# Moving the split weight buffers by 128 bytes in a decoder-layer kernel

## The chip, the core and the metric

The kernel runs on one core of one Trainium2 chip. The metric is the device time of one execution in microseconds (us). TensorE does the matmuls, VectorE (DVE), ScalarE (ACT) and GpSimd (POOL) the elementwise work, SyncE (SP) issues most of the DMAs. All of them read their operands from SBUF, a memory of 128 partitions; where a buffer starts in the bytes of a partition is what is changed here.

## The reference

One hybrid decoder layer over 256 tokens of width 2048, in float32:

```python
proj = h @ w_in                                  # q, k, v, two latents, rope, two gates
y_a = dilated_window_attention(q, k, v) @ a_w_out
y_b = mla_attention(cq @ w_uq, ckv @ w_ukv) @ mla_w_out
mix = (g_a * y_a + g_b * y_b) @ w_out
h = layer_norm(ALPHA * h + mix)
# PEER: product keys choose 16 of 128*128 experts per head, 8 heads
u = expert_down[e];  v = expert_up[e]
y = sum over chosen e of  gate_e * gelu(u . h) * v
h = layer_norm(ALPHA * h + y)
```

The kernel doesn't gather experts. It computes `gelu(h @ down)` for all 16,384 experts, multiplies it by a gate matrix that is zero except at the chosen ones, and multiplies the product by `up`.

## The kernel before, in words

All weights come as one stream of 425 tiles of 128 x 2048 float32, in the order in which they are used: 64 tiles for q, k, v and one gate of each head, 9 for the latents, 16 for the other gate, 32 for the second attention and the first output projection, 16 each for the second output projection, the mixing projection and the query projection, 128 for the down table and 128 for the up table. Each tile is loaded in two halves of 128 x 1024. There are four slots for halves, in three buffers: `raw` is filled by SP's DMA, ScalarE rounds it into `w_hi` (type fp32r) and VectorE writes the rest, `raw - w_hi`, into `w_lo` (line 666). Each slot takes 4096 bytes of a partition.

A product in float32 is made of three fp32r products: hi x hi, lo x hi and hi x lo. In all stages but the last the weights are the stationary operand (128 x 128, loaded by LDWEIGHTS, "PEld" in the profile) and the activations move (256 columns, 258 in the query projection): `three`, line 1115, called 16 times per tile by `full` and 16 times by `up_proj`. That makes 297 tiles x 48 = 14,256 matmuls; these stages are called the dense ones below. In the up stage it is the other way round: the gated activations `m_hi` and `m_lo` are stationary, and 512 columns of `w_hi` or `w_lo` move (`up`, line 1320, and `up_bank` for the last two tiles); that makes 128 x 24 = 3,072 matmuls. Three neighbours in program order differ in which of the three products they are, not in their size. Between the tiles of the attention stages stand the small float32 matmuls and transposes of one head (lines 1149 to 1170).

The order of work is written out by hand for each engine, with semaphores between them. Buffers are laid out in the order of their declaration, each behind the one before. From the sizes follows where each starts. Modulo 512 bytes these places are, before: `raw`, `w_hi`, `w_lo` at 128; `a_hi`, `a_lo`, `res`, `cst` at 64; with the spacer `gap_b` behind `cst`, all buffers of the later stages that TensorE reads (`b_hi`, `b_lo`, `c_hi`, `c_lo`, `head`, `logit`, `p_t`, `v_t`, `qp`, `keys`, `r_hi`, `r_lo`, `m_hi`, `m_lo`) at 64 too. Every operand of a matmul starts a whole multiple of 512 bytes behind the start of its buffer, so these numbers hold for each of them.

Of the kernel before, what the change touches and what calls it, by code (L numbers as in the profile page):

```python
# [24 lines left out]
F32 = mybir.dt.float32  # L25
# [6 lines left out]
P = 128  # L32
# [11 lines left out]
TOPK = 16  # L44
# [32 lines left out]
C_ID = C_ROPE + T  # L77
C_ONE = C_ID + P
C_IOTA = C_ONE + P
C_SLOPE = C_IOTA + P  # L80
C_TOKEN = C_SLOPE + HEADS
N_CONST = C_TOKEN + 16

# [24 lines left out]
class Chain:  # L108
# [5 lines left out]
    def link(self, ins):  # L114
        ins.then_inc(self.sem, 1)
        self.k += 1
        self.eng.wait_ge(self.sem, self.base + self.k)
# [12 lines left out]
def build(nc, stream, x_t, const_in, small_in, keys_t, ln2, y_out, a_dram, g_dram):  # L130
    ctx = ExitStack()

    def sb(name, shape, dt=F32, stack=ctx):
        return stack.enter_context(nc.sbuf_tensor(name, shape, dt))
# [3 lines left out]


    raw = sb("raw", [P, 4, HALF])  # L140
    w_hi = sb("w_hi", [P, 4, HALF], F32R)
    w_lo = sb("w_lo", [P, 4, HALF], F32R)
    small = sb("small", [P, N_SMALL])
    stat = sb("stat", [P, 16])
    carrier = sb("carrier", [P, 16])
    a_hi = sb("a_hi", [P, KD, T], F32R)
    a_lo = sb("a_lo", [P, KD, T], F32R)
    res = sb("res", [P, KD, T])
    cst = sb("cst", [P, N_CONST])
    sb("gap_b", [P, 96])  # L150

    mix_mem = ExitStack()
    b_hi = sb("b_hi", [P, KD, T], F32R, mix_mem)
# [45 lines left out]
    up_mem = ExitStack()  # L199

    a_in = sb("a_in", [P, 2, 4, T], F32, up_mem)
    g_in = sb("g_in", [P, 2, 4, T], F32, up_mem)
    m_f = sb("m_f", [P, 2, T], F32, up_mem)
    m_hi = sb("m_hi", [P, 2, T], F32R, up_mem)
    m_lo = sb("m_lo", [P, 2, T], F32R, up_mem)
# [54 lines left out]
    def col(c, n):  # L260
        return cst[:, c:c + n]
# [3 lines left out]

    ident = col(C_ID, P)
    ones = col(C_ONE, P)
    iota = col(C_IOTA, P)

    def h1_part(b):  # L270

# [382 lines left out]
    def _(dve):  # L654
# [16 lines left out]
        def softmax(a, dilated, h):  # L671
            dve.wait_ge(s_ready, a + 1)
            if dilated:

                link(dve.scalar_tensor_tensor(out=logit[:], in0=col(C_D, 384), scalar=cst[:, bass.ds(h + C_SLOPE, 1)],
                                              in1=col(C_NA, 384), op0=ALU.mult, op1=ALU.add))
# [678 lines left out]
def _constants():  # L1355

    c = np.zeros((P, N_CONST), np.float32)
    for b, (qt, kt) in enumerate(((0, 0), (1, 0), (1, 1))):
        q = np.arange(P)[:, None] + P * qt
        k = np.arange(P)[None, :] + P * kt  # L1360
        d = q - k
        count = np.zeros((P, P), np.float32)
        for window, dilation in PATTERNS:
            count += (d >= 0) & (d <= window) & (d % dilation == 0)
        s = slice(P * b, P * b + P)
        c[:, C_D:][:, s] = -d
        c[:, C_NA:][:, s] = np.where(count > 0, 0.0, NEG)
        c[:, C_NB:][:, s] = np.where(d >= 0, 0.0, NEG)
        c[:, C_C:][:, s] = count
    half = ROPE // 2  # L1370
    inv_freq = np.float32(10000.0) ** (-np.arange(half, dtype=np.float32) / np.float32(half))
    ang = (np.arange(T, dtype=np.float32)[:, None] * inv_freq[None, :]).T
    cos, sin = np.cos(ang), np.sin(ang)
    c[:, C_ROPE:C_ROPE + T] = np.concatenate([cos, cos, -sin, sin])
    c[:, C_ID:C_ID + P] = np.eye(P)
    c[:, C_ONE:C_ONE + P] = 1.0
    c[:, C_IOTA:C_IOTA + P] = np.arange(P)
    c[:, C_TOKEN:C_TOKEN + TT] = np.arange(P)[:, None] + P * np.arange(TT)[None, :]
    c[:, C_SLOPE:C_SLOPE + HEADS] = 2.0 ** (-8.0 * np.arange(1, HEADS + 1) / HEADS)
    return c  # L1380
# [56 lines left out]
```

## Time and profile before

| | |
|---|---|
| median of 3 runs | 2462.61 us (2460.51 to 2463.73) |
| the profiled execution, its time | 2466.07 us |
| its span, first to last instruction | 2464.4 us |
| TensorE matmul busy | 2436.1 us, 99% |
| TensorE weight load busy | 2302.7 us, 93% |
| VectorE busy | 1487.4 us, 60% |
| ScalarE busy | 1166.3 us, 47% |
| GpSimd busy | 554.4 us, 22% |
| mean granted TensorE clock | 0.998 |

A matmul's duration in the profile is the time from its start to the end of its last result; the next one starts long before that, so durations overlap, and the distance from start to start (called the pitch here) is what adds up to the span. The views used are the page itself, the waits of TensorE, the groups of instructions (`x` is the count, then busy us and mean ns), one line's or tile's instructions with least, median and longest duration in ns, the timeline, and the busy time in given stretches.

### The profile page before, as it was taken

Reading aid. Unit: us, or ns where it says so; the run is one execution under the profiler, and the core shown is the slowest. Engines: PE = TensorE matmul, PEld = TensorE weight load, DVE = VectorE, ACT = ScalarE, POOL = GpSimd, SP = SyncE. Lnnn points to the kernel's source line nnn. Section 1 sums busy time; section 2 is a strip of 40 time slices with the busy share of each in tenths; the row PEclk is TensorE's granted clock in tenths of the full one; section 3 lists DMA queues with packets and bytes.
Section 4 is the critical chain, followed back from the end, with each engine's and each line's share of the span. In section 5 each row is a group of like instructions: output and inputs, shape, how many; then the busy total and the mean of one; then the engine's idle time right before and its main releaser. Section 6 shows DMA issues by size and latency. Waiting matters only on the chain.

```text
span 2464.4 us, 49767 instructions
## 1 busy us (share of the span) xinstructions
PE 2436.1 (99%) x17939; PEld 2302.7 (93%) x17940; DVE 1487.4 (60%) x2444; ACT 1166.3 (47%) x1660; POOL 554.4 (22%) x379
## 2 busy tenths in 40 slices
PE   8999999999999999999999999999999999999997
PEld 8999999999999999999999999999888888888886
DVE  5555554546666667688788744444555555555556
ACT  5444444554444444655555544444444444444444
POOL 0000000000000000468888888800000000000000
PEclk9999999999999999999999999999999999999999
DMA  7766766555445655578888888876677777677774
GB/s 267 223 215 225 222 220 198 182 176 156 150 160 170 199 189 184 169 207 211 203 223 218 212 220 219 214 253 218 224 241 240 245 239 230 238 241 244 239 231 144
DMA packets 179845, 521.21 MB, mean 211 GB/s; under 512 B 52768, under 2 KB 52768, under 8 KB 179536
## 3 DMA queue, kind: packets, MB, share of 16 engines
q1 hardware_dynamic: 124128, 449.89, 56.3%
q0 software_dynamic: 51056, 53.89, 10.2%
q10 hardware_dynamic: 4608, 16.78, 1.7%
q8 instruction: 26, 0.43, 0.1%
q14 instruction: 27, 0.22, 0.0%
HBM read 484.70 MB, written 35.78 MB: 211 GB/s over the span
## 4 chain that ended last, share of the span: by engine, by line
PE 98%; DVE 1%; ACT 0%; issue 0%; DMA 0%; ACTq 0%; DVEq 0%
PE ps L1115 66%; PE ps L1320 28%; PE ps L1154 1%; PE ps L1169 1%; PE ps L1162 0%; PE ps L1156 0%; PE ps L1289 0%; PE ps L1170 0%; PE ps L1149 0%; DVE u_s L1068 0%; DVE u_s L1078 0%; DVE y_s L1055 0%; DMA res<-x_t 0%; ACT w_hi L378 0%; DVE w_lo L666 0%
## 5 line engine op out<-in xcount | busy, mean ns | idle before, releaser
L666 DVE TENSOR_TENSOR w_lo<-raw,w_hi 128x1024 fp32r<-128x1024 f32 x850 | 1016.4, 1225 | 736.6 <-ACT w_hi L378 731.4
L1115 PE MATMUL ps<-a_hi,w_hi 128*128 128x256 f32 x3728 | 1044.1, 280 | 10.2 <-DVE w_lo L666 10.2
L1115 PE MATMUL ps<-a_lo,w_hi 128*128 128x256 f32 x3728 | 1035.8, 278 | 0.0
L1115 PE MATMUL ps<-a_hi,w_lo 128*128 128x256 f32 x3728 | 1035.6, 278 | 0.0
L378 ACT ACTIVATE w_hi<-raw 128x1024 fp32r<-128x1024 f32 x850 | 864.9, 1053 | 211.9 <-PE ps L1320 178.0
L1115 PEld LDWEIGHTS ps<-a_hi,w_hi 128*128 128x128 f32 x3728 | 704.5, 189 | 11.1 <-issue 9.1
L1115 PEld LDWEIGHTS ps<-a_hi,w_lo 128*128 128x128 f32 x3728 | 701.8, 188 | 0.0
L1115 PEld LDWEIGHTS ps<-a_lo,w_hi 128*128 128x128 f32 x3728 | 701.0, 188 | 0.5
L349 POOL DMA_INDIRECT g_dram<-gate_v,where x256 | 457.6, 1788 | 114.1 <-issue 81.5
L1320 PE MATMUL ps<-w_lo,m_hi 128*128 128x512 f32 x1008 | 314.1, 393 | 0.0
L1320 PE MATMUL ps<-w_hi,m_hi 128*128 128x512 f32 x1008 | 312.5, 391 | 0.0
L1320 PE MATMUL ps<-w_hi,m_lo 128*128 128x512 f32 x1008 | 311.4, 390 | 0.0
L1320 PEld LDWEIGHTS ps<-w_hi,m_lo 128*128 128x128 f32 x1008 | 189.2, 188 | 43.3
L1320 PEld LDWEIGHTS ps<-w_lo,m_hi 128*128 128x128 f32 x1008 | 189.3, 188 | 40.9
L1320 PEld LDWEIGHTS ps<-w_hi,m_hi 128*128 128x128 f32 x1008 | 189.4, 188 | 40.0
L596 ACT ACTIVATE act<-ps 128x256 f32<-128x256 f32 x128 | 49.2, 384 | 321.5 <-PE ps L1115 320.3
L339 POOL DMA_DIRECT2D a_in<-a_dram x32 | 17.1, 534 | 753.5 <-DVE m_f L1022 749.4
L590 ACT ACTIVATE m_hi<-m_f 128x256 fp32r<-128x256 f32 x128 | 53.4, 417 | 208.9 <-DVE m_f L1022 208.9
L1115 PE MATMUL ps<-b_hi,w_hi 128*128 128x256 f32 x512 | 142.8, 279 | 0.0
L1115 PE MATMUL ps<-b_lo,w_hi 128*128 128x256 f32 x512 | 141.5, 276 | 0.0
L1115 PE MATMUL ps<-b_hi,w_lo 128*128 128x256 f32 x512 | 141.5, 276 | 0.0
L322 POOL DMA_DIRECT2D g_dram<-blank x32 | 24.2, 755 | 360.2 <-DVE w_lo L666 347.5
(187 smaller groups left out, 2098.9 us busy)
## 6 DMA issues: line engine op xcount, KB each, us to landing
raw<-stream SPq DMA_DIRECT2D x850, 512.0 KB, 4.4
g_dram<-blank POOLq DMA_DIRECT2D x32, 512.0 KB, 6.2
a_dram<-act ACTq DMA_DIRECT2D x32, 512.0 KB, 3.7
a_in<-a_dram POOLq DMA_DIRECT2D x32, 512.0 KB, 5.1
g_in<-g_dram POOLq DMA_DIRECT2D x32, 512.0 KB, 6.4
g_dram<-gate_v,where POOLq DMA_INDIRECT x256
res<-x_t SPq DMA_DIRECT2D x4, 512.0 KB, 6.8
ln_s<-ln POOLq DMA_DIRECT2D x1, 2048.0 KB, 7.3
```

The source lines that it names most:

```text
L322: pool.dma_start(g_view[n], blank[:].rearrange("p (o t) -> p o t", o=1).to_broadcast([P, 4, T])).then_inc(g_zero, 16)
L339: pool.dma_start(a_in[:, b], a_dram[i * 2 + b]).then_inc(ag_in[b], 16)
L349: pool.indirect_dma_start(out=g_cell, out_offset=bass.IndirectOffsetOnAxis(ap=where[:, tt, k:k + 1], axis=0), in_=gate_v[:, tt, k:k + 1], ...
L378: act.activation(w_hi[:, t.slot(hf), :], raw[:, t.slot(hf), :], ACT.Copy).then_inc(hi_ready, 1)
L590: act.activation(m_hi[:, par, :], m_f[:, par, :], ACT.Copy).then_inc(mhi_ready, 1)
L596: act.activation(act4[:, b // 4, b % 4, :], acc[t.par][:, 0:T], ACT.Gelu).then_inc(acc_free[t.par], 1)
L666: dve.tensor_tensor(w_lo[:, s, :], raw[:, s, :], w_hi[:, s, :].bitcast(F32), ALU.subtract).then_inc(lo_ready, 1)
L1115: ins = pe.matmul(out, w, a, start=first and q == 0, stop=last and q == 2)
L1154: ins = pe.matmul(ps_s[:, o:o + k1], q_s[:, q0:q0 + P], k_s[:, 0:k1], start=True, stop=not rope)
L1169: pe.matmul(ps_o[:, 0:T], v_s[:, 0, :], p_t[:, 0:T], start=True, stop=False, skip_group_check=True)
L1320: ins = pe.matmul(ps[:, o:o + 512], m[:, b % 2, s], w[:, t.slot(hf), 512 * c:512 * c + 512], start=False, stop=False, skip_group_check=True)
```

## The change

Two spacers are added and two are resized, and a constant table that was longer than its use is cut.

- `gap_w`, 128 bytes, between `raw` and `w_hi`: `w_hi` and `w_lo` start at 256 modulo 512. `raw` stays at 128.
- `gap_a`, 384 bytes, ahead of `a_hi`: `a_hi`, `a_lo`, `res`, `cst` are at 64 again.
- `gap_b` shrinks from 384 to 320 bytes, and the buffers behind it are where they were, at the same addresses.
- `gap_m`, 128 bytes, ahead of `m_f`: `m_f`, `m_hi`, `m_lo`, `zero`, `y_s`, `u_s` are at 192, and what follows them moves along by 128 bytes.
- The row 0, 1, 2, ... in `cst` (`iota`) is 16 long in place of 128. Only its first 16 elements were read before. `cst` shrinks from 8832 to 8384 bytes per partition; `ident` and `ones` ahead of it keep their places, the slopes and token numbers behind it move.

So the distance of the stationary operand's start from the moving one's, modulo 512, goes from +64 to +192 bytes in the dense stages, and is -64 in the up stage before and after. No instruction is added, removed, resized or moved.

```diff
-C_SLOPE = C_IOTA + P
+C_SLOPE = C_IOTA + TOPK
...
     raw = sb("raw", [P, 4, HALF])
+    sb("gap_w", [P, 32])
     w_hi = sb("w_hi", [P, 4, HALF], F32R)
     w_lo = sb("w_lo", [P, 4, HALF], F32R)
     small = sb("small", [P, N_SMALL])
     stat = sb("stat", [P, 16])
     carrier = sb("carrier", [P, 16])
+    sb("gap_a", [P, 96])
     a_hi = sb("a_hi", [P, KD, T], F32R)
     a_lo = sb("a_lo", [P, KD, T], F32R)
     res = sb("res", [P, KD, T])
     cst = sb("cst", [P, N_CONST])
-    sb("gap_b", [P, 96])
+    sb("gap_b", [P, 80])
...
     g_in = sb("g_in", [P, 2, 4, T], F32, up_mem)
+    sb("gap_m", [P, 32], F32, up_mem)
     m_f = sb("m_f", [P, 2, T], F32, up_mem)
...
-    iota = col(C_IOTA, P)
+    iota = col(C_IOTA, TOPK)
...
-    c[:, C_IOTA:C_IOTA + P] = np.arange(P)
+    c[:, C_IOTA:C_IOTA + TOPK] = np.arange(TOPK)
```

## Rows read from the trace of the kernel before

**Rows 1.** The page: busy time by engine, and the chain that ended last.
```profile
PE 2436.1 (99%) x17939; PEld 2302.7 (93%) x17940; DVE 1487.4 (60%) x2444; ACT 1166.3 (47%) x1660; POOL 554.4 (22%) x379
...
PE 98%; DVE 1%; ACT 0%; issue 0%; DMA 0%; ACTq 0%; DVEq 0%
PE ps L1115 66%; PE ps L1320 28%; PE ps L1154 1%; PE ps L1169 1%; PE ps L1162 0%; PE ps L1156 0%; PE ps L1289 0%; PE ps L1170 0%; PE ps L1149 0%; DVE u_s L1068 0%; DVE u_s L1078 0%; DVE y_s L1055 0%; DMA res<-x_t 0%; ACT w_hi L378 0%; DVE w_lo L666 0%
```

**Rows 2.** TensorE's largest wait: us in total, times, longest.
```profile
PE ps L1115 <- DVE w_lo L666: 10.2, 3, 9.1
```

**Rows 3.** Line 1115 by stretch: us, busy us and count, clock, DMA share, GB/s.
```profile
10.00:421.00 411.00, 398.19 (x3310) 386.73 (x3309) 1.00 0.69 224
423.00:548.60 125.60, 124.22 (x1054) 123.99 (x1052) 1.00 0.57 181
550.00:754.00 204.00, 175.43 (x1440) 169.67 (x1440) 1.00 0.49 154
760.50:930.40 169.90, 169.90 (x1501) 169.90 (x1500) 1.00 0.59 193
930.40:1026.00 95.60, 93.66 (x770) 93.02 (x768) 1.00 0.57 182
1039.00:1227.00 188.00, 187.07 (x1584) 186.69 (x1584) 1.00 0.77 202
1227.90:1744.20 516.30, 516.30 (x4557) 516.17 (x4555) 1.00 0.80 222
```

**Rows 4.** Groups of TensorE in 1227.9 to 1744.2 us, the down stage's later part.
```profile
L1115 PE MATMUL ps<-a_lo,w_hi 128*128 128x256 f32 x1519 | 419.2, 276 | 0.0
```

**Rows 5.** The same group in 1039 to 1227 us, the down stage's first part.
```profile
L1115 PE MATMUL ps<-a_lo,w_hi 128*128 128x256 f32 x528 | 148.4, 281 | 0.0
```

**Rows 6.** Groups in 550 to 754 us, the second attention.
```profile
L1115 PE MATMUL ps<-c_lo,w_hi 128*128 128x256 f32 x240 | 67.4, 281 | 0.0
L1115 PE MATMUL ps<-b_lo,w_hi 128*128 128x256 f32 x240 | 66.3, 276 | 0.0
```

**Rows 7.** A group in 10 to 421 us, the first attention; one in 930.4 to 1026.
```profile
L1115 PE MATMUL ps<-a_hi,w_lo 128*128 128x256 f32 x1104 | 307.1, 278 | 0.0
...
L1115 PE MATMUL ps<-r_lo,w_hi 128*128 128x258 f32 x256 | 72.6, 284 | 0.0
```

**Rows 8.** Tile cst: the transposes of line 1297; least, median, longest ns.
```profile
L1297 PEld LDWEIGHTS ps<-cst,res x32: 139/140/144, 1035.5 to 1038.9; 128*128 128x128 f32 x32
L1297 PE MATMUL ps<-cst,res x32: 272/273/273, 1035.6 to 1039.0; 128*128 128x128 f32 x32
```

**Rows 9.** Timeline of TensorE: start us, us from first start to last end.
```profile
1035.64 1.15 PE L1297 MATMUL ps<-cst,res 128*128 128x128 f32 x9
...
93.18 0.59 PE L1169 MATMUL ps<-p_t,head 128*128 128x256 f32 x2
...
2000.18 0.62 PE L1320 MATMUL ps<-w_hi,m_lo 128*128 128x512 f32 x2
2000.64 0.62 PE L1320 MATMUL ps<-w_hi,m_hi 128*128 128x512 f32 x2
```

**Rows 10.** A group in 92 to 96 us.
```profile
L1169 PE MATMUL ps<-p_t,head 128*128 128x256 f32 x2 | 0.6, 377 | 0.0
```

**Rows 11.** Line 1320 in 1999 to 2011 us: least, median, longest ns.
```profile
L1320 PE MATMUL ps<-w_hi,m_lo x18: 388/390/392, 1998.8 to 2010.0; 128*128 128x512 f32 x18
L1320 PEld LDWEIGHTS ps<-w_hi,m_lo x18: 187/188/188, 1998.8 to 2010.9; 128*128 128x128 f32 x18
```

**Rows 12.** Groups of the page and of the whole span: VectorE and ScalarE.
```profile
L666 DVE TENSOR_TENSOR w_lo<-raw,w_hi 128x1024 fp32r<-128x1024 f32 x850 | 1016.4, 1225 | 736.6 <-ACT w_hi L378 731.4
...
L1027 DVE TENSOR_TENSOR m_lo<-m_f,m_hi 128x256 fp32r<-128x256 f32 x128 | 54.4, 425 | 61.9 <-ACT m_hi L590 61.9
```

**Rows 13.** Busy time by stretch: us; PE, PEld, DVE, ACT, POOL; clock, DMA, GB/s.
```profile
1160.00:1260.00 100.00, 99.59 (x856) 99.39 (x856) 82.15 (x245) 54.90 (x71) 85.06 (x50) 1.00 0.82 210
```

**Rows 14.** Tile cst: its first reader on VectorE.
```profile
L675 DVE SCALAR_TENSOR_TENSOR logit<-cst x16: 611/614/614, 31.5 to 389.9; 128x384 f32<-128x384 f32 x16
```

## The prediction

> **What bounds the kernel now.** I read the page first. TensorE is busy 99% of the span and holds 98% of the chain that ended last, 66% in line 1115 and 28% in line 1320 [rows 1]. Its largest wait for another engine is 10.2 us in all, 9.1 of them the first load [rows 2]. So the time is the number of matmuls times their pitch, and a change of layout can act only through the pitch, unless it slows another engine so far that TensorE has to wait.
>
> The pitch isn't one number. Busy time by stretch gives it for the dense matmuls where nothing else stands between: 516.3 us for 4,557 are 113.3 ns, 169.9 us for 1,501 are 113.2 ns, but 188.0 us for 1,584 are 118.7 ns, some of that a few small waits [rows 3]. The durations say the same more sharply: 276 ns in the fast stretch, 281 ns in the slow one, for the same line and the same operands [rows 4, 5]. In the second attention the tiles with `c` are at 281 and those with `b` at 276 [rows 6], the first attention is mixed at 278, the query projection is at 284 with 258 columns [rows 7]. The clock is at its full level of 2.4 GHz in all of them [rows 3].
>
> Next, what would the same work take undisturbed? The transposes of line 1297 move 128 float32 columns, and nine of them take 1.15 us from the first start to the last end [rows 9]; less one duration of 0.273 [rows 8] that leaves 8 pitches of 109.6 ns. In the fast dense stretch duration and pitch stand at 276 and 113.3, each some 4 above 272 and 109.6: the pitch grows by what the duration grows. For the double size, the two matmuls of line 1169 give 0.59 [rows 9] less 0.377 [rows 10] = 213 ns, and twice the transposes' pitch would be 219; take 215. In the up stage two starts are 0.46 us apart, so the pitch is some 229 [rows 9], with durations of 388 to 392 [rows 11]. So each matmul is stretched by something: about 4 ns at the 276 ns level, 9 at the 281 ns one, some 13.5 in the up stage. In all these rows a weight load runs beside the matmul. In line 1297 it is a shorter one (140 ns), in line 1320 it takes 188 [rows 8, 11].
>
> That the stretch depends on how the reading of the stationary operand falls against that of the moving one is my reading of this, not something that a row shows: it fits that one and the same instruction has two steady levels, and that the level changes only where a tile starts after a break. In the trace before, addresses modulo 512 have one relation in the dense stages (+64) and one in the up stage (-64), so no row shows +192.
>
> **The change, part by part.** No instruction comes or goes, so every term is a count times a change of pitch.
>
> Dense stages. I split the 14,256 into those at the slow level and the rest. Slow are 1,054 (423 to 548.6 us), 1,584 (1039 to 1227 us), half of 1,440 in the second attention, the 770 of the query projection [rows 3, 5 to 7], and of the 3,310 in the first attention a share that I take as 1,100: the mean of 278.2 (307.1 / 1,104) lies 0.44 of the way from 276 to 281, and some of that is the start of a tile after a break. That makes 5,230 slow and 9,030 fast. The step between the levels is 4.5 ns (from 5 in the duration, and 118 against 113.3 in the pitch).
> - If with +192 all are fast: 5,230 x 4.5 ns = 23.5 us less.
> - If all are slow: 9,030 x 4.5 = 40.6 us more.
> - If the stretch goes: 9,030 x 3.9 + 5,230 x 8.4 = 35 + 44 = 79 us less.
> - If it is as large as in the up stage, 13.5: 9,030 x 9.5 + 5,230 x 5 = 86 + 26 = 112 us more.
> These are the bounds of the one unknown price. I take the first.
>
> Up stage. Stationary and moving buffer move by 128 bytes alike, so their relation stays. I take 0. If the place itself counted, the bound downwards is 3,072 x 13.5 = 41 us less, and with as much again upwards 41 more; I give it little weight, since the 18 matmuls of one kind there stay within 388 and 392 ns although they read four slots and two halves of `m` [rows 11].
>
> VectorE and ScalarE. Until now all operands of line 666 start at 128; now `raw` does and the others are at 256. Its length law shows nothing lost before: (1225 - 425) / (1024 - 256) = 1.04 ns per column, from two lines at different places [rows 12]. I take 0. If it did get slower, TensorE covers it: in its busiest stretch VectorE works 82% of the time [rows 13]. A tile there takes 48 x 118 ns = 5.7 us, in which line 666 runs twice, 2.45 us, and 1.0 us is free; it would have to grow by two fifths before TensorE's pace followed it. The bound upwards is less than another 10 us of such waits as there are [rows 2], downwards 10 us, if they went.
>
> DMA. `raw`, the target of the stream, doesn't move. `cst` is loaded at the start with 5% fewer bytes, and its first reader on VectorE starts at 31.5 us [rows 14]: 0. The last layer norm works on buffers at 192 now, in instructions of the same size: 0.
>
> Sum against the profiled execution: 2466.1 - 23.5 = 2442.6. That execution is 3.5 us above the median of the runs shown, so against the median of 2462.6 it is 2439. I say 2440.
>
> **The rivals.**
>
> *Nothing happens.* The two levels would then come from something that has nothing to do with where the buffers start, and the time is 2462.6, within 5 us (0.2%, about what a measurement of this kernel can tell from no change). For it speaks that both levels exist at the very same addresses [rows 4, 5]. Against it, that the three kinds of relation that the trace has (the transposes at equal places with their short load, dense, up) each have their own stretch. This is also what the Trainium skill would give: "TensorE: Matmul & The Clock Gate", in the part on the step LDWEIGHTS, says that TensorE has two independent read ports, so that loading the next weights takes nothing from a running matmul. Its gap for back-to-back matmuls ("Back-to-back issue gap" there) would be 109.2 ns for 256 columns; the transposes agree, the dense rows are 4 to 9 ns over it, so the trace doesn't bear the rule out in full, and I leave this case a fifth to a quarter.
>
> *Slower: the 281 ns level takes all.* Whether a stage runs at 276 or 281 is settled at the start of a tile after a break, and then holds for as long as 516 us. With the new relation the reading of the weights falls on another part of the matmul, 128 bytes later; if that level is the only steady one there, the down stage's last 4,557, the 1,501 before 930 us and the fast tiles of the attentions all fall to it: +40.6 us, 2503. It decides from some 1,100 more slow matmuls than now on, which make 5 us. For it speaks that the 276 ns level holds more of the work now, 9,030 against 5,230, so there is more to lose than to gain at this step; against it, that at most tile starts of the first attention it is reached from the other within a few matmuls.
>
> *Slower, and much: the dense stages get the up stage's stretch.* The relation -64 shows 13.5 ns, +64 shows 4 to 9. If +64 is a good spot at which the two reads meet only in part, and the stretch elsewhere is the full one, then it is +112 us, 2575.
>
> *Faster, and much: the stretch goes.* If the distance now keeps the reads apart, -79 us, 2384. For it speaks that the stretch already differs by place; against it, that in a matmul of 256 columns the load of 128 goes on nearly all the time (PEld 93% busy [rows 1]), so they will meet somewhere in each.
>
> **How the numbers follow.** All fast: 0.28. Nothing: 0.22. All slow: 0.22. The up stage's stretch: 0.12. The stretch goes, in part or whole: 0.12. The remaining 0.04 is for something else that costs. Faster by over 0.2%: 0.28 + 0.12 = 0.40, and I add 0.01 from the mixed outcomes: 0.41. Within 0.2%: 0.22. Slower: 0.37. The likeliest case has its own range, 2428 to 2455, because the split by level is an estimate and the level may move by a ns or so. For 8 in 10 the range takes in the other two middle cases, with 2503 at its upper side, and half of the far one below: 2404 to 2506. Left out are the up stage's stretch and the other half of the case where it goes.
>
> **What would show it right or wrong.** Right: the groups of line 1115 at 276 ns in 423 to 549 us, in the tiles with `c`, and from 1039 us on; line 1320 still at 390 to 393; the down stage 7 us shorter, TensorE's waits as they were. Nothing: the same 276 and 281 in the same stretches. Slow: 281 after 1227 us, and the down stage 20 us longer. A duration other than 276 or 281 means that the distance sets its own level, and its difference from 276 times the count is the change. Wrong from the root: line 1320 changed although its relation didn't, or new waits of TensorE for line 666.

## The result, and the profile after

The changed kernel takes longer: median 2497.03 us against 2462.27 us of the kernel before run beside it, ratio 1.0109 with a 95% interval of 1.0066 to 1.0151. Its executions are 2484.28, 2490.18, 2496.41, 2497.65 and 2498.72 us (one more, at a granted clock of 0.66, is left out). The ratio is not the quotient of the two medians, which is 1.0141: the times lie in clusters, and a median sits in one of them. The forecast was 2440, faster.

The profiled execution took 2490.18 us, its span is 24.1 us longer than that of before. The page of the changed kernel, to be read beside [rows 1]; the columns are the same:

```profile
PE 2460.2 (99%) x17939; PEld 2326.7 (93%) x17940; DVE 1486.5 (60%) x2444; ACT 1166.9 (47%) x1660; POOL 542.1 (22%) x379
...
L669 DVE TENSOR_TENSOR w_lo<-raw,w_hi 128x1024 fp32r<-128x1024 f32 x850 | 1016.6, 1225 | 759.6 <-ACT w_hi L381 753.1
```

TensorE is busy 24.1 us longer with the same 17,939 matmuls. VectorE's line (666 before, 669 now) is at 1225 ns as it was [rows 12]. TensorE's largest wait, of the changed kernel, is the one of [rows 2]:

```profile
PE ps L1118 <- DVE w_lo L669: 10.0, 2, 9.0
```

So what has changed is TensorE's pitch. By stretch, for the dense line (1118 now); the columns are those of [rows 3], and the stretches follow the stages, which start a little later:

```profile
10.00:421.00 411.00, 398.27 (x3308) 386.99 (x3308) 1.00 0.69 224
423.00:548.60 125.60, 124.22 (x1053) 124.02 (x1053) 1.00 0.57 181
550.00:754.00 204.00, 176.79 (x1426) 171.13 (x1427) 1.00 0.47 151
764.00:933.70 169.70, 169.70 (x1500) 169.70 (x1499) 1.00 0.60 193
934.00:1028.00 94.00, 92.11 (x769) 91.52 (x767) 1.00 0.57 183
1231.30:1768.00 536.70, 536.70 (x4560) 536.70 (x4558) 1.00 0.76 213
```

The last row is the change: 4,560 matmuls take 536.7 us, 117.7 ns each, where 4,557 took 516.3, 113.3 each [rows 3]. That is 20.4 of the 24.1 us. The first two rows and the fourth are as before. In the third, 14 matmuls fewer fit into the same time: the tiles with `b` have gone to the higher level (280 ns for `b_lo` in place of 276 [rows 6]), some 3 us over the stage. The query projection is some 1.5 us shorter (281 ns in place of 284 [rows 7]). The rest, about 2 us, lies in the short steps between stages and was not followed. Groups of TensorE in 1245 to 1740 us and then in 762 to 925 us of the changed kernel:

```profile
L1118 PE MATMUL ps<-a_hi,w_lo 128*128 128x256 f32 x1401 | 392.3, 280 | 0.0
L1118 PE MATMUL ps<-a_lo,w_hi 128*128 128x256 f32 x1402 | 391.2, 279 | 0.0
...
L1118 PE MATMUL ps<-b_lo,w_hi 128*128 128x256 f32 x230 | 63.5, 276 | 0.0
```

At +192 the lower level is still 276 ns; the higher one shows as 279 and 280 in place of 281 [rows 5], with the same pitch. The up stage, 1772 to 2470 us of the changed kernel, stayed, as its relation did:

```profile
L1323 PE MATMUL ps<-w_lo,m_hi 128*128 128x512 f32 x1006 | 313.5, 393 | 0.0
L1323 PE MATMUL ps<-w_hi,m_lo 128*128 128x512 f32 x1007 | 311.2, 390 | 0.0
```

Where do the two kernels part? Before, TensorE had a break in the down stage at 1226.5 us, and came out of it at the other level. Timeline of TensorE in the kernel before, start in us, the idle time it ends in brackets:

```profile
1226.38 0.28 PE L1115 MATMUL ps<-a_lo,w_hi 128*128 128x256 f32 x1
1226.50 0.28 PE L1115 MATMUL ps<-a_hi,w_lo 128*128 128x256 f32 x1
1227.18 0.39 PE L1115 MATMUL ps<-a_hi,w_hi 128*128 128x256 f32 x1 [0.41 <-DVE w_lo L666]
1227.40 0.28 PE L1115 MATMUL ps<-a_lo,w_hi 128*128 128x256 f32 x1
...
1228.10 0.28 PE L1115 MATMUL ps<-a_lo,w_hi 128*128 128x256 f32 x1
1228.22 0.28 PE L1115 MATMUL ps<-a_hi,w_lo 128*128 128x256 f32 x1
1228.33 0.28 PE L1115 MATMUL ps<-a_hi,w_hi 128*128 128x256 f32 x1
```

The same place in the changed kernel:

```profile
1230.40 0.28 PE L1118 MATMUL ps<-a_lo,w_hi 128*128 128x256 f32 x1
1230.52 0.28 PE L1118 MATMUL ps<-a_hi,w_lo 128*128 128x256 f32 x1
1230.92 0.39 PE L1118 MATMUL ps<-a_hi,w_hi 128*128 128x256 f32 x1
1231.15 0.28 PE L1118 MATMUL ps<-a_lo,w_hi 128*128 128x256 f32 x1
...
1231.97 0.28 PE L1118 MATMUL ps<-a_hi,w_lo 128*128 128x256 f32 x1
1232.09 0.28 PE L1118 MATMUL ps<-a_hi,w_hi 128*128 128x256 f32 x1
```

Both have the break, of 0.68 and 0.40 us from start to start. Before, the matmuls go in steps of 0.12 us and after some six of them in steps of 0.11; in the changed kernel they stay at 0.12, for 537 us.

### The profile page after: what moved, and what is told of

Read it like the earlier page. It is cut to its first block, busy times and chain, and to the rows that moved or that the text cites. A ratio compares the mean times of both kernels' runs of the same rounds, so it can differ in the third digit from the quotient of the medians.

```text
span 2488.5 us, 49767 instructions
## 1 busy us (share of the span) xinstructions
PE 2460.2 (99%) x17939; PEld 2326.7 (93%) x17940; DVE 1486.5 (60%) x2444; ACT 1166.9 (47%) x1660; POOL 542.1 (22%) x379
## 3 DMA queue, kind: packets, MB, share of 16 engines
q0 software_dynamic: 51056, 53.83, 10.2%
## 4 chain that ended last, share of the span: by engine, by line
PE 98%; DVE 1%; issue 0%; ACT 0%; DMA 0%; ACTq 0%; DVEq 0%
PE ps L1118 66%; PE ps L1323 28%; PE ps L1157 1%; PE ps L1172 1%; PE ps L1165 0%; PE ps L1159 0%; PE ps L1292 0%; PE ps L1173 0%; PE ps L1152 0%; DVE u_s L1071 0%; DVE w_lo L669 0%; DVE u_s L1081 0%; DVE y_s L1058 0%; DMA res<-x_t 0%; PE ps L1300 0%
## 5 line engine op out<-in xcount | busy, mean ns | idle before, releaser
L669 DVE TENSOR_TENSOR w_lo<-raw,w_hi 128x1024 fp32r<-128x1024 f32 x850 | 1016.6, 1225 | 759.6 <-ACT w_hi L381 753.1
L352 POOL DMA_INDIRECT g_dram<-gate_v,where x256 | 445.4, 1740 | 113.0 <-issue 78.5
```

What stands on the lines that cost most here:

```text
L352: pool.indirect_dma_start(out=g_cell, out_offset=bass.IndirectOffsetOnAxis(ap=where[:, tt, k:k + 1], axis=0), in_=gate_v[:, tt, k:k + 1], ...
L669: dve.tensor_tensor(w_lo[:, s, :], raw[:, s, :], w_hi[:, s, :].bitcast(F32), ALU.subtract).then_inc(lo_ready, 1)
```

## The experiments

Two questions stood at the start: does the level hang on the distance between the two operands' places, on the places themselves, or only on how a stretch happens to start? The expectations set theories called A and B against each other; each expectation says anew what its two are.

**Which buffer, and distance or place.** Four kernels. `e1_m192` is the kernel before and moves `m` alone:

```diff
+    sb("gap_m", [P, 32], F32, up_mem)
     m_f = sb("m_f", [P, 2, T], F32, up_mem)
```

> The kernel before with only the up stage's activations moved: m at 192, weights at 128, so the up stage's relation is +64 in place of -64. Theory A (the pitch has two levels, 113.3 and 117.8 ns, whatever the distance; which one a stretch gets is settled by how it starts after a break): line 1320 stays at 388 to 394 ns, time 2462 +- 3. Theory B (the distance sets the stretch): the up stage gets the dense stages' 4 to 9 ns, duration 382 to 386, 3,072 x 5 to 9 ns = 15 to 28 us less, 2434 to 2447.

Measured: 2474.93 median of 9, ratio 1.0024 (0.999 to 1.0058), the profiled execution 2494.19. The interval holds no change for the whole kernel; what is shown is the up stage. Groups in 1772 to 2450 us:

```profile
L1321 PE MATMUL ps<-w_hi,m_lo 128*128 128x512 f32 x970 | 305.0, 396 | 0.0
L1321 PE MATMUL ps<-w_lo,m_hi 128*128 128x512 f32 x969 | 304.8, 396 | 0.0
```

396 in place of 390 to 393: the up stage got slower, 500 us hold 2,145 matmuls where they held 2,186, so 4.4 ns each or 13.5 us in all. Neither theory had it; that distance counts, B had right, but with the wrong sign. The profiled execution is some 20 us above most of the others, and that part lies in the down stage, whose distance is still +64. Its dense line by stretch:

```profile
1090.00:1215.00 125.00, 125.00 (x1105) 125.00 (x1105) 1.00 0.84 217
1300.00:1700.00 400.00, 400.00 (x3398) 400.00 (x3398) 1.00 0.79 215
```

Here the first part is at the lower level and the last part at the higher one, the reverse of the kernel before, at the same dense addresses.

`e2_m64` is the changed kernel without `gap_m`: dense +192, up -192.

```diff
-    sb("gap_m", [P, 32], F32, up_mem)
```

> The changed kernel with m back at 64, weights at 256: relation of the up stage -192, dense stages +192 as in the changed kernel. Theory A: as the changed kernel, 2484 to 2499, line 1323 without its spacer at 388 to 394 ns, down stage at 281. Theory B: the up stage's durations leave 388 to 394 one way or the other.

Measured: 2504.39 median of 4 (2482.38 to 2509.01), 1.0139 (1.0083 to 1.0194). The up stage again holds 2,144 in 500 us, so -192 is like +64. In this execution the two output projections, too, are at the higher level, which costs 6.7 us over their 1,500 matmuls; in the profile of the changed kernel they are not. Groups in 762 to 925 us of `e2_m64`:

```profile
L1117 PE MATMUL ps<-a_lo,w_hi 128*128 128x256 f32 x247 | 68.9, 279 | 0.0
L1117 PE MATMUL ps<-b_lo,w_hi 128*128 128x256 f32 x213 | 59.4, 279 | 0.0
```

`e3_all192` moves everything else that TensorE reads along by 128 bytes, so that all distances are those of before:

```diff
     sb("gap_w", [P, 32])
-    sb("gap_a", [P, 96])
-    sb("gap_m", [P, 32], F32, up_mem)
```

> Weights at 256 as in the changed kernel and everything else that TensorE reads at 192, so that all relations are those of the kernel before and only the places moved by 128. Theory B (the distance decides): levels by stretch as in the kernel before, the down stage at 276 from 1227 us on, the tiles with b at 276, 2462 +- 4. Theory A: the levels 276 and 281 exist, and the down stage is at 276 only if TensorE is made to wait for line 666 within it; without such a wait 2482 to 2498.

Measured: 2462.61 median of 10 (2457.84 to 2479.83), 0.9997 (0.9973 to 1.0022): the kernel before, at other places. Dense line by stretch in `e3_all192`:

```profile
1300.00:1700.00 400.00, 400.00 (x3532) 400.00 (x3531) 1.00 0.81 223
```

That is 113.3 ns. This kernel keeps everything of the change (weights at 256, the shorter table, `raw` apart from `w_hi`) except the distances, and has the times of the kernel before: nine of ten executions lie at 2458 to 2465. So the distance decides, not the place. This run alone doesn't refute theory A, since the break of the down stage was there too.

`e4_d0` has weights and dense activations at the same place, 64, and `m` at 0:

```diff
-    sb("gap_w", [P, 32])
+    sb("gap_w", [P, 112])
-    sb("gap_a", [P, 96])
+    sb("gap_a", [P, 16])
-    sb("gap_m", [P, 32], F32, up_mem)
+    sb("gap_m", [P, 112], F32, up_mem)
```

> Weights at 64, activations at 64, m at 0: relation 0 in the dense stages, -64 in the up stage. Theory A: durations of line 1115 only 276 and 281, time 2462 or 2482 to 2498 by whether the down stage is broken by a wait. Theory B: a level of its own other than 276 and 281, or one of them throughout.

Measured: 2536.12 median of 4, all within 0.7 us, 1.0297 (1.027 to 1.0323). One level, 283 ns. Groups in 1280 to 1800 us, and the same line by stretch:

```profile
L1118 PE MATMUL ps<-a_lo,w_hi 128*128 128x256 f32 x1445 | 408.9, 283 | 0.0
```

```profile
465.00:530.00 65.00, 65.00 (x544) 65.00 (x543) 1.00 0.57 180
1300.00:1700.00 400.00, 400.00 (x3335) 400.00 (x3335) 1.00 0.79 211
```

3,335 in 400 us are 119.9 ns. Theory A, that the levels are 276 and 281 whatever the distance, falls with this run.

**All distances.** Eight kernels differ from the changed one in the three spacers alone, as `e4_d0` does. In bytes, `gap_w`, `gap_a`, `gap_m`: `e5_d128_u0` 64, 448, 128; `e6_d256_u128` 192, 320, 384; `e7_d384_u384` 320, 192, 256; `e8_d448_u256` 384, 128, 192; `e13_d32` 480, 32, 64; `e14_d96` 32, 480, 64; `e15_d160` 96, 416, 64; `e16_d224` 160, 352, 320. For the first of them:

```diff
-    sb("gap_w", [P, 32])
+    sb("gap_w", [P, 16])
-    sb("gap_a", [P, 96])
+    sb("gap_a", [P, 112])
```

> Weights at 192, dense activations at 64, m at 192: relation +128 in the dense stages, 0 in the up stage. So far: dense +64 has levels 276 and 281 ns, +192 has 276 and 279 to 280 (pitch 117.8), 0 has 283 alone (pitch 120.0); up -64 has a pitch of 228.9, +64 and -192 have 233.3. Theory A, the distance sets which levels there are, smoothly: +128 lies between +64 and +192 and has the same two, 2460 to 2500; up 0 lies between -64 and +64, 229 to 233. Theory B, only whether the distance is 0 matters for the dense stages: the same two levels, and the up stage the worse for 0, over 233.

> Weights at 320, activations at 64, m at 448: dense +256, up +128. Theory A: further from +64 the lower level gets rarer or vanishes, at most as bad as 120.0 ns: line 1118 at 279 to 283 throughout, 14,256 x 117.8 to 120 against 114.9 now, 2500 to 2536 by the dense stages. Theory B: 276 and 281 as at +64. Up at 233.3 in both.

> Weights at 448, activations at 64, m at 320: dense +384, which is -128, up -128. Theory A: on the far side of 0, near to the single level of 0, 283 ns, 2536 by the dense stages; up between -64 (228.9) and -192 (233.3). Theory B: levels 276 and 281.

> Weights at 0, activations at 64, m at 256: dense -64, up +256. Theory A: next to 0 on the far side; if the dense stages like what the up stage likes, -64 is their best place and the pitch is under 113.3, else it is as 0, 120. Theory B: as +64. Up at 233.3 in both.

> Dense relation +32 (weights at 96), up +32 (m at 128). Lines of 64 bytes: the matmuls behave as at 0 (283 ns, pitch 120.0, 2536 by the dense stages) or as at 64 (276 and 281, 2460 to 2485). Smooth: a level between, 116 to 118 ns, or one under 113.

> Dense +96 (weights at 160), up -32 (m at 128). Lines of 64 bytes: as +64 (276 and 281) or as +128 (279 to 287, 119 to 120 ns, 2518 to 2538). Smooth: between the two.

> Dense +160 (weights at 224), up -96 (m at 128). Lines: as +128 (119 to 120 ns) or as +192 (276 and 279 to 280, 2484 to 2505). Smooth: between. Up: as -64 (228.9) or as -128 (233.3).

> Dense +224 (weights at 288), up +96 (m at 384). Lines: as +192 (276 and 279 to 280) or as +256, which is as 0 (283, 120.0 ns). Smooth: between. Up at 233.3, as +64 and +128 are.

Measured. The dense pitch is 400 us divided by the count in 1300 to 1700 us of each profile (in brackets), the up pitch 500 us by that in 1900 to 2400. A count takes in the two or so matmuls that reach over the ends of the stretch, so the quotient comes out some 0.1 ns low here, and 0.25 ns low in a stretch of 125 us: from start to start the levels are 113.3, 117.8 and 120.0 ns. The times are medians of two to four executions, but for the rows before and after.

| kernel | time, us | dense distance | dense pitch, ns | up distance | up pitch, ns |
|---|---|---|---|---|---|
| `e4_d0` | 2536.1 | 0 | 119.9 (3,335) | -64 | 228.7 (2,186) |
| `e13_d32` | 2526.7 | 32 | 118.3 (3,382) | 32 | 233.1 (2,145) |
| before | 2462.3 | 64 | 113.3 (3,532) | -64 | 228.7 (2,186) |
| `e14_d96` | 2518.1 | 96 | 117.3 (3,411) | -32 | 233.2 (2,144) |
| `e5_d128_u0` | 2517.8 | 128 | 118.6 (3,373) | 0 | 226.4 (2,208) |
| `e15_d160` | 2549.3 | 160 | 119.9 (3,336) | -96 | 233.1 (2,145) |
| after | 2497.0 | 192 | 117.7 (3,398) | -64 | 228.6 (2,187) |
| `e16_d224` | 2512.1 | 224 | 117.7 (3,399) | 96 | 234.1 (2,136) |
| `e6_d256_u128` | 2550.0 | 256 | 119.9 (3,335) | 128 | 233.2 (2,144) |
| `e7_d384_u384` | 2538.6 | 384 | 118.6 (3,373) | -128 | 233.2 (2,144) |
| `e8_d448_u256` | 2483.1 | 448 | 117.7 (3,399) | 256 | 226.6 (2,207) |

(Besides 64 and 192, two more distances show two levels. `e16_d224` was at 116.5 before the break of the down stage, 1,073 in 125 us; `e5_d128_u0` holds 544 in 465 to 530 us, the same as `e4_d0` there.) Two rows of the many, first `e6_d256_u128`, to be held against `e4_d0`, then `e7_d384_u384`, whose count is that of `e5_d128_u0`:

```profile
1300.00:1700.00 400.00, 400.00 (x3335) 400.00 (x3335) 1.00 0.78 210
```

```profile
1300.00:1700.00 400.00, 400.00 (x3373) 400.00 (x3372) 1.00 0.79 214
```

The table repeats after 256 bytes, in both stages: 0 and 256, 128 and 384, 192 and 448 agree, and so do up 0 and 256, +64 and -192. The times of such pairs differ by what the up stage differs: `e6` is 14 us over `e4`, and 3,072 x 4.5 ns are 13.8 us. The up stage also shows once more that the place doesn't count: a distance of 0 modulo 256 was tried with weights and `m` at 192 and 192, 0 and 256, and 128 and 128 (`e12_m128` below), always 226.4 to 226.6. The dense pitch changes at steps of 32 bytes too (119.9, 118.3, 113.3, 117.3 from 0 to 96), though some distances share one, as 0 and 160 do. So theory B of the first four of these expectations (only 0 is bad, all else like +64) is wrong, and so is a count by 64-byte lines; a smooth course, their theory A, is wrong as well, since 160 has 119.9 and lies between 128 with 118.6 and 192 with 113.3 or 117.7. That -64 might be the dense stages' best place (`e8`) is wrong as well: it is -64, which is 192 modulo 256, and behaves as the changed kernel does. Only 64 and 192 modulo 256 showed 113.3 ns at all. The up stage's best distance is 0, which no expectation had.

**The start, or the odds.** At +64 and at +192 two levels exist, 113.3 and 117.7 ns. Two kernels tried to choose the level by what stands ahead of the down stage's tiles 1 and 33. Both unroll eight tiles of TensorE's loop twice and call this ahead of the second tile of each:

```python
        def small():
            pe.wait_ge(ht_ready, 8)
            pe.matmul(spare[0][:, 0:T], qp[:, 0, 0:P], qp[:, 1, :], start=True, stop=True)
            pe.matmul(spare[0][:, P:T], qp[:, 2, 0:P], qp[:, 3, 0:P], start=True, stop=True)
```

In `e9_after_small` on the changed kernel; in `e10_before_turn` on the kernel before, with two transposes of `qp` by `ident` in place of the matmuls.

> The changed kernel, with two small float32 matmuls (256 and 128 columns, results unused) ahead of the down stage's tiles 1 and 33, so that those tiles start as the first attention's third tile of a head does, which runs at 276 ns at +192 as well as at +64. Theory A (the distance offers the levels, the start picks one, and the change costs time because the down stage picks 281 and its like): down stage at 276, 6,100 x 4.45 ns = 27 us less, 1.3 us more for the small ones: 2462 to 2471. Theory B (at +192 a long stretch can't hold the lower level in this stage): 279 to 280 as in the changed kernel, 2485 to 2499.

Measured: 2496.8 median of 5, 1.0125 (1.0082 to 1.0169), but the profiled execution took 2478.11. Its dense line:

```profile
1090.00:1215.00 125.00, 125.00 (x1064) 125.00 (x1063) 1.00 0.81 211
1300.00:1700.00 400.00, 400.00 (x3532) 400.00 (x3531) 1.00 0.80 223
```

In that execution the stretch before 1215 us is at the higher level and the one after 1300 at the lower, at +192. So +192 can hold the lower level for the whole rest of the stage; theory B falls. But by their times, 2495 to 2498, four of five executions didn't get it: the small matmuls don't choose.

> The kernel before, with two float32 transposes (results unused) ahead of the down stage's tiles 1 and 33, so that they start as the first attention's first tile of a head does, which runs at 281 ns. Theory A: with no address moved, the down stage runs at 281 throughout, 4,550 x 4.45 = 20 us more: 2483. Theory B (the place decides and the start doesn't): 2463.

Measured: 2465.41 median of 10, 1.0021 (0.9988 to 1.0054). Six executions lie at 2459 to 2466 and four at 2480 to 2487; the profiled one is of the four, with the addresses of the kernel before (rows of `e10_before_turn`):

```profile
1300.00:1700.00 400.00, 400.00 (x3398) 400.00 (x3398) 1.00 0.77 215
```

That is 117.7 ns, the pitch of the changed kernel. It is 20 us more without any address moved, but not in all executions: the start as I made it doesn't decide either. What remains are odds: executions of one and the same kernel differ. Of the 73 executions of the kernel before in all these comparisons, 62 lie at 2458 to 2470 us and 11 at 2479 to 2485. To have the same for the changed kernel, it was run again as it is (`e17_after_again`, no edit).

> The changed kernel once more, unchanged, for the spread of its executions. If +192 holds the lower level in the down stage as easily as +64 (some 8 in 10 there), most executions lie near 2464 to 2478; if it does so rarely, most lie at 2484 to 2499 with one in some ten 20 us lower.

Measured: 2470.32, 2489.35, 2495.78, 2496.78, 2496.82, 2498.36; 1.0118 (1.0078 to 1.0158). With the first five that is one of 11 below 2484. Its profiled execution (2489.35) shows the draw at each break, dense line by stretch:

```profile
1090.00:1215.00 125.00, 125.00 (x1106) 125.00 (x1105) 1.00 0.84 221
1300.00:1700.00 400.00, 400.00 (x3399) 400.00 (x3398) 1.00 0.78 214
```

The lower level stands before the break and the higher one after it, the reverse of `e9_after_small`. At +192 modulo 256 (with `e2`, `e8` and `e9`) 3 of 23 executions lie where the lower level in the last part of the down stage puts them: 2470.32, 2478.11 and 2482.38; only the second was profiled. For the first and the third the level is read from the time alone.

The output projections show a second turn. In all seven profiles with a dense distance of +64 (before, `e1`, `e3`, `e10`, `e11`, `e12`, `e18`) they are at the lower level. At +192 modulo 256 they are so in two of five (the changed kernel, `e8`) and at the higher one in `e2`, `e9` and `e17`. The row of `e17_after_again`:

```profile
775.00:930.00 155.00, 155.00 (x1318) 155.00 (x1317) 1.00 0.57 186
```

**A kernel that may beat both.** The up stage's best distance with the dense stages' best: the kernel before with `m` at 128 (`e12_m128`, and once more as `e18_m128_again`); `e11_m128_small` has the small matmuls as well.

```diff
+    sb("gap_m", [P, 16], F32, up_mem)
     m_f = sb("m_f", [P, 2, T], F32, up_mem)
```

> The kernel before with m at 128 alone. The up stage's pitch goes from 228.9 to 226.7 ns by its own relation, whatever the dense one is: 2455.5. If up and dense stages hang together by the places themselves and not by the distance: 2462 or more.

> The kernel before, m at 128 (relation 0 in the up stage, pitch 226.7 seen at 0 and at +256) and the two small matmuls ahead of tiles 1 and 33. Theory A: up stage 3,072 x 2.2 = 6.8 us less, the down stage all at 276, 1,584 x 4.45 = 7 us less, 1.3 more: 2450. Theory B: the small matmuls do nothing, 2457.

> The kernel before with m at 128, once more: executions in two clusters, 2453 to 2459 and 2472 to 2479, each 6 to 7 us under those of the kernel before (2458 to 2466 and 2479 to 2485), by 3,072 matmuls x 2.2 ns.

Measured: `e12` 2458.54 median of 10, 0.9989 (0.9955 to 1.0023); `e11` 2458.8, 0.9971 (0.9939 to 1.0003); `e18` 2454.67 median of 12, 0.9981 (0.9958 to 1.0004). The up stage does what was expected, groups in 1772 to 2440 us of `e12_m128`:

```profile
L1321 PE MATMUL ps<-w_hi,m_lo 128*128 128x512 f32 x983 | 302.7, 389 | 0.0
L1321 PE MATMUL ps<-w_lo,m_hi 128*128 128x512 f32 x982 | 302.3, 389 | 0.0
```

389 against 390 to 393, and 226.4 ns against 228.7. In `e18` ten executions lie at 2451 to 2458 and two at 2474 to 2476; of `e12` six and four. The intervals hold no change, since the 20 us steps swamp the 7; the up stage's own gain is plain in the profiles, a gain of the whole is likely and not shown. The small matmuls add nothing that can be told.

## Why the prediction was wrong

The bound was right: TensorE's pitch is the time, and the sum of counts times levels holds. With the two levels of the trace of before, 4,560 x 4.4 = 20 us for the down stage's last part, 720 x 4.4 = 3 us for the tiles with `b` and -1.5 us for the query projection give 21.5 of the 24.1 us. With the output projections at the higher level too, as in `e2_m64`, it is 1,500 x 4.45 = 6.7 us more, 2497, where most executions lie; `e17_after_again` shows that the changed kernel does this too.

The step that failed is the choice in "Dense stages", "I take the first", all at 276. The rival "the 281 ns level takes all", +40.6 us, named the mechanism, the level and the stretch that moved; its size was off, since 9,030 was to move and 5,300 did in the profile, and by the times 6,800 in most executions. I had weighed it under the other on no row: the trace shows both levels at +64 and nothing at +192, so it couldn't choose. The sign that the prediction had named, a duration other than 276 or 281, came: 279 and 280. The measured 2497 lies within the wide range only because that range took in this rival's 2503. What the trace did show, and I didn't use, is how uneven the stake was. One break at 1226.5 us had put 4,557 matmuls at the lower level, half of all that was there: there was much to lose at this step and little to win.

Behind it lies a second error. I took the levels of one profiled execution for those of the kernel. They are drawn anew at breaks: the kernel before itself takes 20 us more in 11 of 73 executions. The three times shown before were all of the lower cluster. What the change does is to turn the odds of the lower level in the down stage's last part, by the times from 62 of 73 to 1 of 11. That it does so by the distance is shown by `e3_all192`, nine of ten at the distances of before.

Point by point. That the reading of both operands meets, and that each distance has its own stretch: the distances bear it out, though some share one (`e3_all192` at the same distances equals before, `e4_d0` to `e16_d224` differ), while where in the chip they meet is not shown. By the Trainium skill's rule, in "TensorE: Matmul & The Clock Gate", step LDWEIGHTS under "Step-by-step: what each phase is for", the two reads have ports of their own and a weight load takes nothing from the running matmul. That would have given 2462.6 for all of these; measured are 2462 to 2550, so the pair of streams isn't free of each other here. Whether each has a port of its own no run shows, and no run leaves the weight load out. No change in the up stage: right, 390 and 393. None for `w_lo` on VectorE: right, 1225 ns. No new wait: right, 10.0 us in all where it was 10.2. The query projection was counted among the slow at 4.5 ns each, 3.5 us, and gained 1.5. "The stretch goes": not at any distance tried; 113.3 is the lowest. Its floor of 109.6 was read from float32 transposes of 128 columns, and no run shows it for the dense matmuls. "The dense stages get the up stage's stretch", 2575: no distance reached it, 120.0 is the highest seen.

Left open: why the changed kernel rarely comes out of a break at the lower level, and by what the draw is decided. Neither the two kinds of instruction put ahead nor the mere presence of a break does it. Nor is it that a longer or a shorter break gives one level: at +64 the lower one came after 0.68 and 1.79 us (before, `e18`) and the higher one after 0.88 and 1.13 (`e12`, `e1`), from start to start.

## What to carry to other kernels

Where TensorE is the bound and a weight load runs beside each matmul, the distance of the two operands' start addresses modulo 256 bytes is a setting worth up to 3.5% here: look at the matmul's duration in the groups, stage by stage, and move a buffer with a spacer. Read several executions before such a choice, since one kernel can have two levels with 4% between their pitches, each held for half a millisecond, and a single profile shows one draw. And when a layout is moved, count how much of the time now sits at the better level: that is what can be lost.

## What the runs showed of the hardware that was not expected

- fp32r matmuls of 256 columns with a load of 128 beside each: 113.3 or 117.8 ns at distances of 64 and 192 modulo 256, 116.5 to 120.0 at all others tried, with stationary minus moving counted. With 512 columns moving: 226.5 at 0, 228.7 at -64, 233 to 234 at all others tried.
- The two levels at one distance have the same instructions, addresses and clock. In the down stage of the twelve profiles with a dense distance of 64 or 192 modulo 256, a stretch keeps its level over up to 4,559 matmuls and changes it only at a break, of 0.3 to 1.8 us from start to start.
- The up stage, whose matmuls are twice as long, has one level per distance in all profiles.
